# One more small load at the head of ScalarE's queue in a transformer layer of 256 tokens: columns of w_in into an unused tile

## The chip, the cores and the metric

One core of a Trainium2 chip. The metric is the kernel's time on the device in microseconds, the median of several runs; less is better. The kernel before takes 307.39 us (three runs, 307.19 to 308.2).

## What is computed

One decoder layer in float32, for a sequence of 256 tokens and 1024 features: a root-mean-square norm, attention with 16 heads of 64, a residual, a second norm, a squared-ReLU network of width 4096, a residual and a last norm. With 256 tokens the block-sparse attention of the reference has a single block, so that it is plain causal attention with a bias by distance. The reference, cut to this case:

```
y = rmsnorm(x, norm_mix)
q, k, v = split(y @ w_in, 3)                 # w_in: 1024 x 3072, float32
s = q @ k.T * 64 ** -0.5 + rel_bias[bucket(t - s)]     # per head, causal
h = x + (softmax(s) @ v) @ w_out
h = h + square(relu(rmsnorm(h, norm_mlp) @ mlp_up)) @ mlp_down
out = rmsnorm(h, final_norm)
```

## The kernel before

Every engine has its program written out by hand, with semaphores between them. The weights (w_in 12 MB, w_out 4 MB, mlp_up and mlp_down 16 MB each) come in tiles of 1 MB into four slots of `raw`, loaded by SyncE's queue (`load`, L209). ScalarE rounds each tile to a high part (`w_hi`, L604), VectorE takes the rest (`w_lo`, L808), and TensorE multiplies high by high and low, and low by high. The attention goes in four chunks of four heads, the network in sixteen chunks of 256 columns.

The order at the start is what matters here. SyncE issues the first 128 rows of x in two halves (L215, semaphores `x_half`), then the first tile of w_in, the columns of v, in four pieces of 256 KB (L220, `v_piece`), with the other 128 rows of x (L218, `x_next`) between the second and third, and then the next tile in two halves (L222, L223) and whole tiles (L209). ScalarE issues three small loads before its first work: `mix_rows` (the gain of the first norm, 8 x 128, L689), `onehot_sb` (L690) and `rel_sb` (L691), both tables for the bias. Then it loads an activation table (L692), and squares x for the norm (L694, L697).

TensorE begins with three products of constants that nobody reads (`idle_product`, L528), each recorded as two passes. It transposes four blocks of x (L292, which waits for `x_half[0]`), then the gains (L287, which waits for `mix_loaded`), then four more blocks (`x_half[1]`). VectorE copies the turned gains to `mixT` (L997) and multiplies the transposed x by them into `yF` (L884). With `yF` and the first piece of w_in TensorE starts v's first tile (`v_first`, L340); the table product L328 and the norm's factor (L300) come between its steps.

Quoted, the start of ScalarE's program and the wait in TensorE's transposes:

```
nc.scalar.dma_start(mix_rows[:], norm_mix[0].rearrange("(k p) -> k p", p=P)).then_inc(mix_loaded, 16)
nc.scalar.dma_start(onehot_sb[:], bucket_onehot).then_inc(tables_loaded, 16)
nc.scalar.dma_start(rel_sb[:], rel_bias).then_inc(tables_loaded, 16)
nc.scalar.preload_act_table(ACT.Sqrt)
act.wait_ge(x_half[0], 16)
...
    if tb == 0 and k == 4:
        pe.wait_ge(mix_loaded, 16)
        nc.tensor.transpose(bank[MIX][:, 0:KB], mix_rows[:], ident[0:KB, 0:KB]).then_inc(mix_turned, 1)
```

Of the kernel before, what the change touches and what calls it, by code (L numbers as in the profile page):

```python
# [31 lines left out]
P = 128  # L32
D = 1024
# [50 lines left out]
def build(nc, x, rel_bias, norm_mix, norm_mlp, mlp_up, mlp_down, w_in, w_out, final_norm,  # L84
# [9 lines left out]
    with ExitStack() as ctx:  # L94
        def sb(name, shape, dt=F32):
            return ctx.enter_context(nc.sbuf_tensor(name, shape, dt))

        def sem(name):
            return ctx.enter_context(nc.semaphore(name))
# [16 lines left out]
        oT = sb("oT", [P, PAIRS, 2, T], F32R)  # L116
        yF = sb("yF", [P, KB, T])
        warm = sb("warm", [P, 256])
        part = sb("part", [P, 2, T])
        z_sb = sb("z_sb", [P, 2, T])  # L120
        s_sb = sb("s_sb", [P, 2, T])
# [40 lines left out]
        bias_summed, bias_vec, bias_stored = sem("bias_summed"), sem("bias_vec"), sem("bias_stored")  # L162
        v_piece = [sem(f"v_piece{i}") for i in range(PIECES - 1)]
        q_first, fill_loaded, yf_done = sem("q_first"), sem("fill_loaded"), sem("yf_done")
        warm_made, sd_done = sem("warm_made"), sem("sd_done")
        square0_act, eps_made = sem("square0_act"), sem("eps_made")
        diag_done, spread_done, yn_done, ylo0_pool = sem("diag_done"), sem("spread_done"), sem("yn_done"), sem("ylo0_pool")
        hi_done, lo_done = sem("hi_done"), sem("lo_done")
# [18 lines left out]
        def cols(slot_tensor, slot):  # L187
            return slot_tensor[:, slot, :].rearrange("p (k n) -> p k n", k=KB)
# [13 lines left out]
        @block.sync  # L202
        def _(sp):
            def load(slot, src, split):

                if split is not None:
                    sp.wait_ge(lo_done, split)
                n = CE // src.shape[1]
                nc.sync.dma_start(raw[:, slot, :].rearrange("p (k n) -> p k n", n=n), src  # L209
                                  ).then_inc(raw_full[slot], 16)  # L210


            for b in range(2):
                own = slice(b * 512, (b + 1) * 512)
                nc.sync.dma_start(h_sb[:, 0, own], x_rows[0][:, own]).then_inc(x_half[b], 16)  # L215
            for i in range(PIECES):
                if i == 2:
                    nc.sync.dma_start(h_sb[:, 1, :], x_rows[1]).then_inc(x_next, 16)  # L218
                ks = slice(i * KB // PIECES, (i + 1) * KB // PIECES)
                nc.sync.dma_start(cols(raw, 0)[:, ks, :], w_in_v[:, ks, 2 * D:2 * D + CW]  # L220
                                  ).then_inc(v_piece[i] if i < PIECES - 1 else raw_full[0], 16)
            nc.sync.dma_start(cols(raw, 1)[:, 0:4, :], w_in_v[:, 0:4, 0:CW]).then_inc(q_first, 16)  # L222
            nc.sync.dma_start(cols(raw, 1)[:, 4:8, :], w_in_v[:, 4:8, 0:CW]).then_inc(raw_full[1], 16)  # L223
            for t, (c, part) in enumerate(IN_PARTS):
                if t > WHOLE:
                    own = slice(PART_BASE[part] + c * CW, PART_BASE[part] + (c + 1) * CW)
                    if t == SLOTS:
                        sp.wait_ge(unit_done, TB)
                    load(t % SLOTS, w_in_v[:, :, own], 2 * (t - SLOTS - WHOLE) + 2 if t > SLOTS else None)
            for q in range(CHUNKS_OUT):  # L230
                load(q, w_out_v[:, 2 * q:2 * q + 2, :], 2 * (OUT0 + q - SLOTS - WHOLE) + 2)
            with sp.Fori(0, CHUNKS_UP // 2) as i:
                for r in range(2):
                    load(2 * r, up_v[:, :, bass.ds(i * 2 * CW + r * CW, CW)], 8 * i + SPLIT0 - 6 + 4 * r)
                    load(2 * r + 1, down_v[:, bass.ds(i * 4 + 2 * r, 2), :], 8 * i + SPLIT0 - 4 + 4 * r)
            for tb in range(TB):
                for b in range(2):
                    own = slice(b * 512, (b + 1) * 512)
                    sp.wait_ge(out_ready, 2 * tb + b + 1)
                    nc.sync.dma_start(out_rows[tb][:, own], y_sb[:, tb, own]).then_inc(stored, 16)  # L240
            sp.wait_ge(stored, 16 * 2 * TB)
            sp.wait_ge(bias_stored, 16)


        @block.gpsimd
# [350 lines left out]
        def _(act):  # L596
# [77 lines left out]
            def h_hi(f, par, i):  # L674
                act.wait_ge(s_done, 2 * f + i + 1)
                nc.scalar.copy(hT[:, par, i, HI, :], s_sb[:, i, :]).then_inc(hhi_done, 1)  # L676

            def step(f, par, first=False, last=False):
# [4 lines left out]
                for i in range(2):  # L683
# [2 lines left out]
                        hi_mlp(f + 2, par, 0, i, (up_done, 2 * f + 2))  # L686
                    h_hi(f + 1, 1 - par, i)

            nc.scalar.dma_start(mix_rows[:], norm_mix[0].rearrange("(k p) -> k p", p=P)).then_inc(mix_loaded, 16)  # L689
            nc.scalar.dma_start(onehot_sb[:], bucket_onehot).then_inc(tables_loaded, 16)  # L690
            nc.scalar.dma_start(rel_sb[:], rel_bias).then_inc(tables_loaded, 16)  # L691
# [36 lines left out]
            for c in range(1, CHUNKS_IN):  # L728
                a, t = c - 1, 3 * c + 3
# [24 lines left out]
            a = CHUNKS_IN - 1  # L754
# [370 lines left out]
```

## Time and profile before

| | |
|---|---|
| median of 3 runs | 307.39 us (307.19 to 308.2) |
| the profiled execution | 306.87 us |
| its span, first to last instruction | 305.1 us |
| busy: TensorE, VectorE, ScalarE | 295.0, 205.8, 158.1 us |
| bytes moved | 55.86 MB, mean 183 GB/s |
| first product with weights (L340) | starts at 6.09 us |

The page is of one execution. Times in a view count from the first instruction of the span. Instructions that issue a transfer have an engine name with a q (ACTq, SPq); a transfer's landing is the moment when its semaphore is full. In the time lines a row merges neighbouring instructions of one line; "x6" is how many, and the brackets tell how long the engine idled before, and what ended that.

### The profile page before, as it was taken

To read this page: it belongs to the slowest core of one execution; us is meant where nothing else is said; L and a number is where in the kernel's file an instruction comes from. 1 tells how busy PE (TensorE), PEld (TensorE's weight loads), DVE (VectorE), ACT (ScalarE), POOL (GpSimd) and SP (SyncE) were. 2 spreads that over 40 slices of the span, in tenths; PEclk is the share of its full clock that TensorE was granted. 3 is DMA by queue.
4 is the path that set the end of the run, shared out by engine and by line. 5 is a ranking of instruction groups with operands and counts; after the bars stand their busy time and mean duration, and the time that the engine had idled before them with its cause. 6 is when DMAs were issued, how large, how long until landed. Compare 5 with 4: busy or idle time off the path is not lost.

```text
span 305.1 us, 4557 instructions
## 1 busy us (share of the span) xinstructions
PE 295.0 (97%) x1645; PEld 251.4 (82%) x1645; DVE 205.8 (67%) x396; ACT 158.1 (52%) x291; POOL 8.4 (3%) x15
## 2 busy tenths in 40 slices
PE   7979989999999999999999999999999999999992
PEld 5868888898997787888888888888888888888881
DVE  2696985984875757894674675666567467466564
ACT  3694753944935545745544545346355354444422
POOL 0401000000000000000000000000000000000000
PEclk9999999999999999999999999999999999999997
DMA  6999977257166044486566547647457556620003
GB/s 231 353 348 354 354 236 265 81 146 268 70 187 227 0 140 138 175 267 183 195 213 178 202 172 221 190 148 259 143 171 242 146 195 209 182 93 0 0 3 136
DMA packets 36685, 55.86 MB, mean 183 GB/s; under 512 B 1144, under 2 KB 29888, under 8 KB 36672
## 3 DMA queue, kind: packets, MB, share of 16 engines
q1 hardware_dynamic: 35632, 52.43, 53.2%
q0 software_dynamic: 928, 3.20, 2.9%
q8 instruction: 8, 0.13, 0.2%
q10 hardware_dynamic: 112, 0.06, 0.1%
q14 instruction: 5, 0.04, 0.0%
HBM read 54.61 MB, written 1.07 MB: 182 GB/s over the span
## 4 chain that ended last, share of the span: by engine, by line
PE 89%; DVE 4%; ACT 3%; DMA 1%; issue 1%; SPq 0%; DVEq 0%; ACTq 0%
PE bank L442 36%; PE bank L391 25%; PE bank L398 13%; PE bank L353 2%; PE bank L354 2%; PE bank L355 2%; PE bank L418 2%; PE bank L340 2%; DVE w_lo L808 2%; DMA raw<-in_a_w_in_dram 1%; PE bank L494 1%; PE bank L432 1%; ACT w_hi L604 1%; PE bank L410 1%; PE bank L408 1%
## 5 line engine op out<-in xcount | busy, mean ns | idle before, releaser
L808 DVE TENSOR_TENSOR w_lo<-raw,w_hi 128x1024 fp32r<-128x1024 f32 x94 | 112.8, 1221 | 40.6 <-ACT w_hi L604 39.5
L604 ACT CAST w_hi<-raw 128x1024 fp32r<-128x1024 f32 x93 | 95.3, 1052 | 32.7 <-PE bank L442 32.6
L391 PE MATMUL bank<-yT,w_hi 128*128 128x512 f32 x352 | 85.8, 392 | 2.4 <-DVE qT L904 2.4
L391 PEld LDWEIGHTS bank<-yT,w_hi 128*128 128x128 f32 x352 | 65.0, 188 | 16.6 <-issue 2.0
L442 PE MATMUL bank<-w_hi,hT 128*128 128x512 f32 x256 | 71.8, 390 | 0.0
L442 PEld LDWEIGHTS bank<-w_hi,hT 128*128 128x128 f32 x256 | 47.1, 188 | 9.0
L398 PEld LDWEIGHTS bank<-yT,w_lo 128*128 128x128 f32 x352 | 46.2, 191 | 2.4
L398 PE MATMUL bank<-yT,w_lo 128*128 128x256 f32 x352 | 46.9, 282 | 0.0
L442 PE MATMUL bank<-w_lo,hT 128*128 128x512 f32 x128 | 40.2, 390 | 0.0
L672 ACT COPY part<-bank 128x256 f32<-128x256 f32 x32 | 11.9, 370 | 36.7 <-PE bank L398 36.7
L442 PEld LDWEIGHTS bank<-w_lo,hT 128*128 128x128 f32 x128 | 24.0, 188 | 5.2
L974 DVE TENSOR_TENSOR z_sb<-bank,part 128x256 f32<-128x256 f32 x32 | 13.5, 422 | 20.3 <-ACT part L672 20.2
L676 ACT CAST hT<-s_sb 128x256 fp32r<-128x256 f32 x32 | 13.1, 408 | 15.2 <-DVE s_sb L976 15.2
L442 PE MATMUL bank<-w_hi,oT 128*128 128x512 f32 x64 | 19.8, 399 | 0.0
L660 ACT ACTIVATE probs<-probs,negmax 128x128 f32<-128x128 f32 (+1 forms) x32 | 14.2, 447 | 10.2 <-DVE negmax L913 10.1
L913 DVE CUSTOM_DVE_ANT_0 probs<-bank,bias_sb 128x128 f32<-128x128 f32 (+1 forms) x32 | 9.7, 350 | 8.1 <-PE bank L410 8.1
L981 DVE TENSOR_TENSOR hT<-s_sb,hT 128x256 fp32r<-128x256 f32 x32 | 13.5, 420 | 1.9 <-ACT hT L676 1.9
L976 DVE SCALAR_TENSOR_TENSOR s_sb<-z_sb 128x256 f32<-128x256 f32 x32 | 13.6, 425 | 1.1
L442 PEld LDWEIGHTS bank<-w_hi,oT 128*128 128x128 f32 x64 | 11.7, 188 | 3.0 <-issue 0.8
L353 PE MATMUL bank<-w_hi,yT 128*128 128x256 f32 x48 | 13.7, 285 | 0.0
L354 PE MATMUL bank<-w_lo,yT 128*128 128x256 f32 x48 | 13.6, 283 | 0.0
L355 PE MATMUL bank<-w_hi,yT 128*128 128x256 f32 x48 | 13.6, 283 | 0.0
(95 smaller groups left out, 238.5 us busy)
## 6 DMA issues: line engine op xcount, KB each, us to landing
raw<-in_mlp_up_dram SPq DMA_DIRECT2D x16, 1024.0 KB, 5.5
raw<-in_mlp_down_dram SPq DMA_DIRECT2D x16, 1024.0 KB, 4.9
raw<-in_a_w_in_dram SPq DMA_DIRECT2D x10, 1024.0 KB, 7.6
raw<-in_a_w_out_dram SPq DMA_DIRECT2D x4, 1024.0 KB, 4.9
bias_sb<-bias_by_distance POOLq DMA_DIRECT2D x4, 512.0 KB, 5.3
raw<-in_a_w_in_dram SPq DMA_DIRECT2D x4, 256.0 KB, 5.1
raw<-in_a_w_in_dram SPq DMA_DIRECT2D x2, 512.0 KB, 7.5
out_dram<-y_sb SPq DMA_DIRECT2D x4, 256.0 KB, 2.3
```

The lines of the kernel that those rows point to most:

```text
L353: mm(acc, yT[:, k, HI, tok], wh[:, k, :], start=(k == 0), stop=False)
L354: mm(acc, yT[:, k, HI, tok], wl[:, k, :], start=False, stop=False)
L355: last = mm(acc, yT[:, k, LO, tok], wh[:, k, :], start=False, stop=(k == KB - 1))
L391: mm(dst[:], wh[:, k, i * P:(i + 1) * P], yT[:, k, :, :], start=(k == 0), stop=False, skip_group_check=True)
L398: last = mm(dst[:, 0:T], wl[:, k, i * P:(i + 1) * P], yT[:, k, HI, :], start=False, stop=(k == KB - 1), skip_group_check=True)
L442: last = mm(bank[ACC[tb][c]][:], lhs(l), w[:, r, c * 512:(c + 1) * 512], start=first, stop=(stop and l == LO))
L604: nc.scalar.copy(w_hi[:, slot, part_of], raw[:, slot, part_of]).then_inc(hi_done, 1)
L660: last = nc.scalar.activation(probs[:, s, own], probs[:, s, own], ACT.Exp, bias=negmax[:, s, tb:tb + 1], scale=-1.0, accum_out=rowsum[:, s ...
L808: v.tensor_tensor(w_lo[:, slot, own], raw[:, slot, own], f32(w_hi[:, slot, own]), ALU.subtract).then_inc(lo_done, 1)
L974: v.tensor_tensor(z_sb[:, i, :], bank[UP[i]][:, 0:T], part[:, i, :], ALU.add).then_inc(z_done, 1)
L976: v.scalar_tensor_tensor(s_sb[:, i, :], z_sb[:, i, :], 0.0, z_sb[:, i, :], ALU.max, ALU.mult).then_inc(s_done, 1)
L981: v.tensor_tensor(hT[:, par, i, LO, :], s_sb[:, i, :], f32(hT[:, par, i, HI, :]), ALU.subtract).then_inc(hT_ready, 1)
```

## The change

It adds one load as the first on ScalarE's queue. It reads 16 columns (64 bytes), from column 2048 on, of rows 0, 4, 8, ... of w_in: 256 runs of 64 bytes, 16 KB, two of them to each of the 128 partitions of a new tile `touch` that nothing reads. SyncE waits for its semaphore at the very end. The three loads that stood first on the queue follow it; no other instruction moves. The rows of w_in are 12 KB long, so that the runs lie 48 KB apart and span the whole array.

```diff
+        touch = sb("touch", [P, 2, 16])
...
-        warm_made, sd_done = sem("warm_made"), sem("sd_done")
+        warm_made, sd_done, touched = sem("warm_made"), sem("sd_done"), sem("touched")
...
             sp.wait_ge(bias_stored, 16)
+            sp.wait_ge(touched, 16)
...
+            every_fourth = w_in[0].rearrange("(p a r) n -> p a r n", a=2, r=4)[:, :, 0, 2 * D:2 * D + 16]
+            nc.scalar.dma_start(touch[:], every_fourth).then_inc(touched, 16)
             nc.scalar.dma_start(mix_rows[:], norm_mix[0].rearrange("(k p) -> k p", p=P)).then_inc(mix_loaded, 16)
```

ScalarE's program at its start, before the change:

```order
0 L595 UNCONDITIONAL_BRANCH
1 L689 DMA mix_rows<-in_norm_mix_dram 8x128
2 L690 DMA onehot_sb<-in_bucket_onehot_dram 32x384
3 L691 DMA rel_sb<-in_rel_bias_dram 32x16
4 L692 ACT_TABLE_LOAD
5 L694 ACTIVATE squares,stat<-h_sb 128x512
```

The same place with the change:

```order
0 L597 UNCONDITIONAL_BRANCH
1 L692 DMA touch<-in_a_w_in_dram 128x2x16
2 L693 DMA mix_rows<-in_norm_mix_dram 8x128
3 L694 DMA onehot_sb<-in_bucket_onehot_dram 32x384
4 L695 DMA rel_sb<-in_rel_bias_dram 32x16
5 L696 ACT_TABLE_LOAD
6 L698 ACTIVATE squares,stat<-h_sb 128x512
```

The load of `touch` stands ahead of the others, and everything behind it has moved down by one; the lines of the file are two or four higher.

## Rows read from the trace of the kernel before

**Rows 1.** The page: busy time by engine, and the chain by engine.
```profile
PE 295.0 (97%) x1645; PEld 251.4 (82%) x1645; DVE 205.8 (67%) x396; ACT 158.1 (52%) x291; POOL 8.4 (3%) x15
...
PE 89%; DVE 4%; ACT 3%; DMA 1%; issue 1%; SPq 0%; DVEq 0%; ACTq 0%
```

**Rows 2.** The chain in order of time: start us, us, what.
```profile
1.27 0.42 SPq L215
1.69 0.05 issue
1.74 4.21 DMA raw<-in_a_w_in_dram
5.95 0.14 issue
6.09 1.10 PE bank L340 x4
...
12.68 0.23 PE bank L300 x2
12.91 0.02 issue
12.94 0.70 DVE y_sb L876
```

**Rows 3.** Time line of ScalarE: start us, us, instruction [idle before].
```profile
0.81 0.60 ACTq L689 DMA_DIRECT2D mix_rows<-in_norm_mix_dram  x1
1.80 0.43 ACTq L691 DMA_DIRECT2D rel_sb<-in_rel_bias_dram  x1
2.26 1.28 ACT L692 ACT_TABLE_LOAD   x1 [2.26 <-issue]
3.56 0.63 ACT L694 ACTIVATE squares<-h_sb 128x512 f32<-128x512 f32 x1
4.09 0.19 ACT L694 ACTIVATION_READ_ACCUMULATOR squares<-h_sb 128x1 f32 x1
4.86 0.63 ACT L697 ACTIVATE squares<-h_sb 128x512 f32<-128x512 f32 x1 [0.58 <-DMA h_sb<-in_x_dram]
```

**Rows 4.** Time line of TensorE's products.
```profile
1.27 2.93 PE L528 MATMUL bank<-warm 128*128 128x256 f32 x6 [1.27 <-DVE warm L993]
3.99 0.91 PE L292 MATMUL bank<-ident,h_sb 128*128 128x128 f32 x4
4.83 0.22 PE L287 MATMUL bank<-ident,mix_rows 8*128 8x8 f32 x1
4.98 0.66 PE L292 MATMUL bank<-ident,h_sb 128*128 128x128 f32 x4
6.09 1.10 PE L340 MATMUL bank<-raw,yF 128*128 128x256 f32 x4 [0.45 <-DMA raw<-in_a_w_in_dram]
7.12 0.81 PE L328 MATMUL bank<-onehot_sb,rel_sb 32*16 32x384 f32 x2
7.86 1.13 PE L340 MATMUL bank<-raw,yF 128*128 128x256 f32 x4
...
9.05 1.04 PE L292 MATMUL bank<-ident,h_sb 128*128 128x128 f32 x8
...
9.92 2.76 PE L340 MATMUL bank<-raw,yF 128*128 128x256 f32 x12
```

**Rows 5.** Time line of VectorE, and the tile yF.
```profile
5.17 0.17 DVE L997 COPY mixT<-bank 128x8 f32<-128x8 f32 x1 [3.94 <-PE bank L287]
5.25 0.14 DVE L999 TENSOR_SCALAR stat<-stat 128x1 f32<-128x1 f32 x1
5.37 1.35 DVE L884 TENSOR_TENSOR yF<-bank,mixT 128x256 f32<-128x256 f32 x3
...
L884 DVE TENSOR_TENSOR yF<-bank,mixT x3: 414/424/681, 5.4 to 6.0; 128x256 f32<-128x256 f32 x2, 128x512 f32<-128x512 f32 x1
```

**Rows 6.** Issues: SyncE's, landings of h_sb, onehot_sb and rel_sb (KB, us to landing).
```profile
0.82 0.87 SPq L215 DMA_DIRECT2D h_sb<-in_x_dram  x2
1.74 0.94 SPq L220 DMA_DIRECT2D raw<-in_a_w_in_dram  x2
...
DMA to landing us min/median/max: 2.7/3.6/5.6
...
onehot_sb<-in_bucket_onehot_dram ACTq DMA_DIRECT2D x1, 48.0 KB, 3.1
...
rel_sb<-in_rel_bias_dram ACTq DMA_DIRECT2D x1, 2.0 KB, 3.9
```

**Rows 7.** ScalarE's queue (q10): packets, MB, share; 1.5:2.6, 2.8:4.0, 4.0:6.0 us.
```profile
q10 hardware_dynamic: 16, 0.00, 1.5%
...
q10 hardware_dynamic: 46, 0.05, 15.9%
...
q10 hardware_dynamic: 50, 0.00, 1.8%
```

**Rows 8.** Stretches: us, busy per engine, PEclk, DMA share, GB/s.
```profile
3.50:4.50 1.00, 1.00 (x5) 0.70 (x4) 0.00 (x0) 0.77 (x3) 0.00 (x0) 1.00 0.72 191
...
5.50:6.50 1.00, 0.55 (x4) 0.42 (x3) 1.00 (x3) 0.38 (x2) 0.00 (x0) 1.00 1.08 377
...
8.50:9.50 1.00, 1.00 (x10) 0.95 (x9) 0.25 (x1) 1.00 (x2) 0.68 (x1) 1.00 1.08 381
```

## The prediction

> **What bounds the kernel now.** I read the page's chain first, since a small load can only matter where something waits for it. The chain is TensorE work for 89% of the span, and DMA has 1% [rows 1]. In order of time, that 1% is one piece: the first 256 KB of w_in, issued at 1.74 us and landed 4.21 us later, at 5.95 us [rows 2]. Behind it the products of L340 start at 6.09 us, and from there each piece of the chain is engine work that hangs on the one before: PE to 12.91, then DVE, ACT, and so on. No transfer is in the chain again in this stretch. So whatever moves the start of L340 should move the end by about as much, and a transfer that comes in later than it does now costs nothing until it passes the work that waits for it.
>
> The next views are the time lines of the three engines before 6.09 us. ScalarE issues three small loads from 0.81 us, loads a table until 3.54, squares the first half row of x from 3.56 to 4.28, then idles 0.58 us for the second half, until 4.86 [rows 3]. TensorE works on the unused products of L528 until about 4.0, starts the first four transposes at 3.99, turns mix_rows at 4.83, starts four more transposes at 4.98, and L340 at 6.09 [rows 4]. VectorE copies mixT at 5.17 and makes the first yF at 5.37; it has three of those, the short ones 0.41 to 0.42 us each, so the first is done near 5.8 [rows 5]. Two things therefore meet before L340: the weights at 5.95 and yF at about 5.8. They lie 0.15 us apart.
>
> **The change, part by part.** It removes and moves no computation. It adds one issue at the head of ScalarE's queue, its packets, and a last wait on SyncE.
>
> *The issue.* The load has 128 x 2 runs of 64 bytes, 256 in all, the same number of runs as the 256 KB pieces of w_in, two of which take SyncE 0.94 us, so 0.47 us each [rows 6]. The first issue of ScalarE's queue takes 0.60 us though it has eight runs [rows 3]. The touch takes that place, so I bound it by 0.47 and 0.9 us and take 0.6. What is behind it on ScalarE moves by 0.35 to 0.6 us: mix_rows is issued near 1.4 instead of 0.81, the table load ends near 4.0 instead of 3.54, the first squares end near 4.75 instead of 4.28. The 0.58 us in which ScalarE waits for x at 4.86 covers this. Cost on the path: 0. If the cover were gone, the squares would feed VectorE's L999 at 5.25, and beyond a delay of about 0.6 us the path.
>
> *The packets.* The load goes over the same 16 engines that carry x and w_in. The small packets of ScalarE's queue between 4.0 and 6.0 us are rel_sb's 64-byte runs, the same size as the touch's: 50 packets have 1.8% of 16 x 2.0 us, 11.5 ns each. Between 2.8 and 4.0 us that queue has 46 packets, mostly onehot_sb's, at 15.9% of 16 x 1.2 us, 66 ns each [rows 7]. So 256 packets and their 16 signals cost each engine 272 x 11.5 / 16 = 0.2 us at the low end and 272 x 66 / 16 = 1.1 us at the high end. I take 0.3 us, close to the row with the same packet size. Who is late by it: the first half row of x lands at 0.82 + 2.7 = 3.5 us [rows 3, 6] while TensorE is on L528 until 3.99, so 0.45 us of it are hidden. The second half lands at 4.86, with its transposes at 4.98: these would start 0.2 us later, and they end at 5.64 today, 0.45 us before L340. Nothing shows. The first piece of w_in would land at 6.25 instead of 5.95, and this does show: +0.3 us.
>
> *What the touch may give back.* It reads from every fourth row of w_in, hence all over the array, before the pieces do. The first pieces come slowly: between 3.5 and 4.5 us the engines move 191 GB/s at a share of 0.72, against 377 GB/s between 5.5 and 6.5 and 381 between 8.5 and 9.5 [rows 8]. The missing bytes of that microsecond are 1.0 x (377 - 191) / 377 = 0.5 us of transfer. If the slowness belongs to the first reads of that array, the touch takes some of it on itself, ahead of the pieces. The trace cannot say so: it may as well be the order in which the transfers were issued. Bounds: 0 and -0.5 us for the landing. But yF at 5.8 allows L340 to start only some 0.2 us sooner than now. I take -0.2 of the 0.3 above.
>
> *mix_rows.* It is now behind the touch on its queue. Today its eight packets and their eight signals are through before 2.6 us, since the queue's 16 packets by then are theirs [rows 7]. Moved by 0.6 us of issue and 0.2 to 1.1 us of touch, they are through between 3.4 and 4.3. TensorE wants them at 4.83. The other row, onehot_sb with 3.1 us from issue to landing [rows 6], gives 1.4 + 3.1 + 0.2 to 1.1 = 4.7 to 5.6 us: up to 0.8 us late, and VectorE's mixT and yF, which wait for it, as late. Eight packets are nearer to their own row, so I take 0, and keep +0.8 as the upper end.
>
> The Trainium skill's page DMA: Bandwidth & Descriptors, Queues, rings and completion order, says that each DMA engine goes round robin over the queues with work. By that rule x would alternate with the touch, where I have charged x the touch's whole time. The Trainium skill's same page, Bandwidth, lists 4 KB in 64 packets at 0.68 us, 10.5 ns a packet, for GpSimd's loads; by this figure 256 packets would be an estimated 2.7 us in a row and mix_rows would be late by a few tenths. No row here has so many tiny packets in one load.
>
> *The rest.* rel_sb lands at 1.80 + 3.9 = 5.7 us and L328 reads it at 7.12 [rows 3, 4, 6]; 1.4 us of cover, against 0.8 at most. The wait of SyncE at the end is for a load that will be 300 us old: 0. The unused tile costs 128 bytes a partition.
>
> **Sum.** +0.3 - 0.2 + 0 = +0.1 us on a profiled execution of 306.87 us (span 305.1), which is 0.5 below the median of 307.39. On the median: 307.5 us. A difference under 0.3%, 0.9 us, cannot be told from none for this kernel.
>
> **The rivals.**
> 1. *mix_rows comes late (slower if late enough).* Its place is the wait before L287, its price one for one through mixT, yF and L340. At 5.6 us it gives +0.8 - 0.1, about 308.2, still inside 0.3%. It decides past 5.8 us: then TensorE has more than 0.9 us of idling. For it: it stands behind 256 packets on one queue. Against: its own packets are gone today 2.2 us before they are wanted. Chance 0.13, of which 0.05 lands beyond 0.3%.
> 2. *TensorE's clock rises later (slower).* The first 256-column products cost 2.93 / 6 = 0.49 us each, those from 9.92 us 2.76 / 12 = 0.23; eight transposes take 1.04 us at 9.05, where the first four alone take 0.91 [rows 4]. So the engine starts at the lower of its two levels, 1.2 GHz, and rises to 2.4 between 4 and 5 us, after being busy since 1.27 without a gap. If x lands more than 0.45 us late, a gap opens at 4.0, and the rise may be put off. From 4.98 to 8.99 stand 0.66 + 1.10 + 0.81 + 1.13 = 3.7 us of work that would take up to twice as long; half of this stretch gives +1.8, less 0.3 of idling that absorbs it: about 308.9 us. It decides from a gap at 4.0 us that keeps the clock low. Chance 0.08. The Trainium skill's TensorE: Matmul & The Clock Gate, Part 1, adds that the chip's looks at activity are not tied to a kernel's start, so the same start may rise earlier or later by chance; the sum would not change by it.
> 3. *The touch pays (faster).* First pieces of w_in land up to 0.5 us sooner. VectorE's yF then caps the gain near 0.2 us, 307.2 us. To pass 0.3%, the later stages would have to wait for DMA too, and the chain holds 1% of DMA, all in that one piece. Chance 0.15, of which 0.04 for more than 0.3%.
> 4. *It does nothing*: the load runs wholly in gaps, or ahead of everything; 307.4 us. Chance 0.14.
>
> The forecast itself has a chance of 0.50.
>
> **How the numbers follow.** 307.5 us. Below, -0.2 from rival 3 and 0.5 for how single medians fall: 306.8. Above, rival 1 at its end and part of rival 2: 308.8. The runs shown span 307.19 to 308.2, so the width is mostly theirs. Faster: 0.04. Slower: 0.05 + 0.08 + 0.01 for a stray median = 0.14. Same: 0.82.
>
> **What would show it.** Right: in the changed profile the first L340 starts between 5.9 and 6.4 us; L287 starts near 4.8; mixT follows it; L528 still runs into the transposes with no gap; ScalarE's idling before its second squares shrinks from 0.58 to about 0.1 us; the rest of the chain is the old one, shifted. Wrong: L287 waits for DMA (rival 1); twelve products of L340 not at 0.23 us at their first group (rival 2); or a start of L340 within 0.2 us of 6.09 and yet an end moved by over 0.9 us, which would mean that the stage behind it depends on the landings in a way that the chain hides.

## The result, and the profile after

The changed kernel takes 309.23 us (six runs, 309.03 to 313.3) against 307.26 us (six runs, 306.75 to 308.2): a ratio of 1.0102 with a 95% interval of 1.0062 to 1.0141. Two of the six runs, 313.16 and 313.3 us, raise that ratio (the last section comes back to them); the two medians alone stand at 1.0064. By them it is slower by 2 us, and outside the forecast range of 306.8 to 308.8. The profiled execution took 309.03 us where the one before took 306.87, and its span is 307.3 us where it was 305.1. So the 2.2 us between the two profiled executions lie inside the span.

The loss does not arise at the start, where the load is. The chain after, in order of time (start us, us, what):

```profile
5.25 0.78 PE bank L294 x4
6.03 0.01 issue
6.04 1.13 PE bank L342 x4
...
12.92 0.70 DVE y_sb L880
```

The first products with weights start at 6.04 us where they started at 6.09, and VectorE begins at 12.92 where it began at 12.94 [rows 2]. No DMA is left in this stretch of the chain. The two chains then run side by side, piece for piece, and the changed one stays 0.01 to 0.06 us ahead, until 128 us. The network begins there. Before:

```profile
128.62 3.69 PE bank L391 x16
132.32 1.91 PE bank L398 x16
134.23 5.47 PE bank L442 x24
139.70 3.63 PE bank L391 x16
143.32 1.91 PE bank L398 x16
145.24 5.47 PE bank L442 x24
...
288.34 10.92 PE bank L442 x48
```

After:

```profile
128.56 3.72 PE bank L393 x16
132.28 1.91 PE bank L400 x16
134.19 5.58 PE bank L444 x24
139.77 3.66 PE bank L393 x16
143.42 1.91 PE bank L400 x16
145.34 5.58 PE bank L444 x24
...
290.26 11.17 PE bank L444 x48
```

Each product has two operands: a stationary one of 128 columns, which the profile shows as a weight load of its own, 128x128 (PEld), and a moving one of 256 or 512. Each step of the network is a group of wide products of the first matrix, 512 columns of the moving operand yT (L391, now L393), narrow ones, 256 columns of it (L398, L400), and 24 products of the second matrix, with hT stationary and 512 columns of the weights moving (L442, L444). The 24 take 5.58 us where they took 5.47, the 16 take 3.66 where they took 3.63, so a step takes 11.15 us (5.58 + 3.66 + 1.91) instead of 11.01; the last 48 take 0.25 us more. The first chain reaches the last 48 at 288.34 us, the second at 290.26. These 1.92 us, and 0.25 on top, are the whole loss. The page says the same of the groups. Before, then after (busy us, mean ns of one):

```profile
L442 PE MATMUL bank<-w_hi,hT 128*128 128x512 f32 x256 | 71.8, 390 | 0.0
...
L442 PE MATMUL bank<-w_lo,hT 128*128 128x512 f32 x128 | 40.2, 390 | 0.0
...
L442 PE MATMUL bank<-w_hi,oT 128*128 128x512 f32 x64 | 19.8, 399 | 0.0
```

```profile
L444 PE MATMUL bank<-w_hi,hT 128*128 128x512 f32 x256 | 73.1, 395 | 0.0
...
L444 PE MATMUL bank<-w_lo,hT 128*128 128x512 f32 x128 | 40.5, 392 | 0.0
...
L444 PE MATMUL bank<-w_hi,oT 128*128 128x512 f32 x64 | 19.8, 399 | 0.0
```

The products that read hT are slower, and those of the same line that read oT are not. TensorE waits for nothing in either. What tells the two tiles apart in the diff is the declaration of `touch`: it stands between `warm` and `part`, so part, z_sb, s_sb, hT and all tiles behind them move up by 128 bytes in each partition, and oT, yT, raw, w_hi and w_lo stay. In the program as built, the tiles follow each other without gaps. All that TensorE's wide products read (yT, w_hi, w_lo, oT, hT) start at 128 modulo 256 bytes before the change, that is, their address divided by 256 leaves 128; hT starts at 0 modulo 256 after it.

At the start, what the prediction asked to look at. ScalarE after:

```profile
0.83 0.64 ACTq L692 DMA_DIRECT2D touch<-in_a_w_in_dram  x1
1.50 0.74 ACTq L693 DMA_DIRECT2D mix_rows<-in_norm_mix_dram  x1
...
3.17 1.28 ACT L696 ACT_TABLE_LOAD   x1 [3.17 <-issue]
4.46 0.63 ACT L698 ACTIVATE squares<-h_sb 128x512 f32<-128x512 f32 x1
...
5.09 0.61 ACT L701 ACTIVATE squares<-h_sb 128x512 f32<-128x512 f32 x1
```

And the DMA view after: ScalarE's queue between 2.8 and 4.0 us, and the landing of the touch.

```profile
q10 hardware_dynamic: 280, 0.02, 20.1%
...
touch<-in_a_w_in_dram ACTq DMA_DIRECT2D x1, 16.0 KB, 3.1
```

In [rows 3] the table load began at 2.26 and ScalarE idled 0.58 us before its second squares; now it begins at 3.17, and the idling is gone. In [rows 7] the queue had 16 packets between 1.5 and 2.6 us; now it has none there, and its 280 between 2.8 and 4.0 us are nearly all the touch's (256 runs and 16 signals), 13.8 ns each (20.1% of 16 x 1.2 us over 280).

### The profile page after: what moved, and what is told of

It is laid out like the page before. It is cut to its first block, busy times and chain, and to the rows that moved or that the text cites. A ratio compares the mean times of both kernels' runs of the same rounds, so it can differ in the third digit from the quotient of the medians.

```text
span 307.3 us, 4558 instructions
## 1 busy us (share of the span) xinstructions
PE 297.6 (97%) x1645; PEld 251.8 (82%) x1645; DVE 205.8 (67%) x396; ACT 157.5 (51%) x291; POOL 8.4 (3%) x15
## 4 chain that ended last, share of the span: by engine, by line
PE 91%; DVE 4%; ACT 3%; issue 1%; DVEq 0%; ACTq 0%
PE bank L444 36%; PE bank L393 25%; PE bank L400 13%; PE bank L355 2%; PE bank L356 2%; PE bank L357 2%; PE bank L420 2%; PE bank L342 2%; DVE w_lo L812 2%; PE bank L496 1%; PE bank L434 1%; ACT w_hi L606 1%; PE bank L530 1%; PE bank L412 1%; PE bank L294 1%
## 5 line engine op out<-in xcount | busy, mean ns | idle before, releaser
L393 PE MATMUL bank<-yT,w_hi 128*128 128x512 f32 x352 | 86.3, 393 | 2.3 <-DVE qT L908 2.3
L393 PEld LDWEIGHTS bank<-yT,w_hi 128*128 128x128 f32 x352 | 64.9, 188 | 17.2 <-issue 2.0
L444 PE MATMUL bank<-w_hi,hT 128*128 128x512 f32 x256 | 73.1, 395 | 0.0
L444 PEld LDWEIGHTS bank<-w_hi,hT 128*128 128x128 f32 x256 | 47.2, 189 | 9.8
L400 PEld LDWEIGHTS bank<-yT,w_lo 128*128 128x128 f32 x352 | 46.2, 191 | 2.4
L400 PE MATMUL bank<-yT,w_lo 128*128 128x256 f32 x352 | 46.9, 282 | 0.0
L444 PE MATMUL bank<-w_lo,hT 128*128 128x512 f32 x128 | 40.5, 392 | 0.0
L444 PEld LDWEIGHTS bank<-w_lo,hT 128*128 128x128 f32 x128 | 24.1, 188 | 5.7
L444 PE MATMUL bank<-w_hi,oT 128*128 128x512 f32 x64 | 19.8, 399 | 0.0
L444 PEld LDWEIGHTS bank<-w_hi,oT 128*128 128x128 f32 x64 | 11.7, 188 | 3.0 <-issue 0.8
L355 PE MATMUL bank<-w_hi,yT 128*128 128x256 f32 x48 | 13.7, 285 | 0.0
L357 PE MATMUL bank<-w_hi,yT 128*128 128x256 f32 x48 | 13.6, 283 | 0.0
```

Of the source, the lines that this page charges most:

```text
L355: mm(acc, yT[:, k, HI, tok], wh[:, k, :], start=(k == 0), stop=False)
L357: last = mm(acc, yT[:, k, LO, tok], wh[:, k, :], start=False, stop=(k == KB - 1))
L393: mm(dst[:], wh[:, k, i * P:(i + 1) * P], yT[:, k, :, :], start=(k == 0), stop=False, skip_group_check=True)
L400: last = mm(dst[:, 0:T], wl[:, k, i * P:(i + 1) * P], yT[:, k, HI, :], start=False, stop=(k == KB - 1), skip_group_check=True)
L444: last = mm(bank[ACC[tb][c]][:], lhs(l), w[:, r, c * 512:(c + 1) * 512], start=first, stop=(stop and l == LO))
```

## The experiments

The theories after the result. *Place*: the tile, not the load, costs the 2 us, because hT is moved. *Load*: the transfer, its issue or the longer program costs them, in a way that the chain does not show.

**The tile without the load.** The tile as in the change, none of its other lines.

```diff
         warm = sb("warm", [P, 256])
+        touch = sb("touch", [P, 2, 16])
         part = sb("part", [P, 2, T])
```

> The unused tile of 128 bytes a partition stands where the change put it, but there is no load and no wait. Theory 'place' (the tile moves part, z_sb, s_sb, hT and all later tiles up by 128 bytes, and the products L444 that read hT get slower, 24 in 5.58 us where they were 24 in 5.47): 309.2 us, the products at 5.58 again. Theory 'load' (the transfer, its issue or the longer program costs the 2 us): 307.3 us and 5.47.

Measured: 309.64 us, ratio 1.0072 (1.0055 to 1.0089), and 24 products in 5.58 us again:

```profile
144.26 3.66 PE bank L392 x16
...
149.83 5.58 PE bank L443 x24
```

Its profiled execution took 313.52 us; the last section shows where that time went.

**The load with the tile last.** The whole change, `touch` declared behind `stat`.

```diff
-        touch = sb("touch", [P, 2, 16])
...
         stat = sb("stat", [P, 6, 6])
+        touch = sb("touch", [P, 2, 16])
```

> The whole change, but with the tile declared last, so that no other tile moves. Theory 'place': 307.3 us or, by the earlier start of the first products, 0.1 less; 24 products in 5.47 us. Theory 'load': 309.2 us and 5.58.

Measured: 307.45 us, ratio 1.0012 (0.9993 to 1.0031), 24 products in 5.47 us:

```profile
145.24 5.47 PE bank L444 x24
150.71 3.63 PE bank L393 x16
```

These two runs settle it between the theories: the tile's place costs the 2 us, and the load costs nothing inside the span, whose median is 305.15 us in these ten runs and 305.4 in the nineteen of the kernel before beside them. But four of the ten took 307.9 to 308.5 and one 308.83. In these five, 2.5 to 2.9 us of the time lie outside the span, and in the other five 1.7 or 1.8. The same was seen without the load, 2.5 us in two of the nineteen runs before and in the single run with hT moved by 256 bytes below, and in none of the six runs of the change itself. What this extra microsecond is, and whether the load makes it more frequent, was not shown.

**Which of the moved tiles.** A pad of 128 bytes behind s_sb moves hT and not part, z_sb and s_sb. With hT declared first, and the pad before `part`, these three stand off and hT does not. The tiles declared behind them all (`gain` and on) stand off by 128 bytes in both kernels.

```diff
         s_sb = sb("s_sb", [P, 2, T])
+        pad = sb("pad", [P, 32])
         hT = sb("hT", [P, 2, 2, 2, T], F32R)
```

> No load; a pad of 128 bytes stands between s_sb and hT, so that hT and what is behind it move and part, z_sb and s_sb do not. Theory 'place, hT': 309.2 us. Theory 'place, part/z_sb/s_sb' (ScalarE's and VectorE's accesses to these slow TensorE down): 307.3 us. Theory 'load': 307.3.

```diff
+        hT = sb("hT", [P, 2, 2, 2, T], F32R)
+        pad = sb("pad", [P, 32])
         part = sb("part", [P, 2, T])
...
-        hT = sb("hT", [P, 2, 2, 2, T], F32R)
```

> No load; hT is declared before the pad and part, z_sb and s_sb behind it, so that these three lie 128 bytes off (and 8 KB up) while hT keeps its place modulo 2048 bytes. Theory 'place, hT': 307.3 us. Theory 'place, part/z_sb/s_sb': 309.2 us. Theory 'load': 307.3.

Measured: 309.47 us, ratio 1.0074 (1.0052 to 1.0097), for hT; 307.01 us, ratio 0.9995 (0.9986 to 1.0005), for the others. The 24 products, with hT off and then with the others off:

```profile
146.07 5.58 PE bank L443 x24
```

```profile
145.09 5.47 PE bank L443 x24
```

It is hT. The tiles behind it are off in the fast kernel too, and so are ruled out.

**How far.** The same pad with other sizes (16 columns, as shown, are 64 bytes; 64 and 256 columns are 256 and 1024), and the output projection's tile oT moved by 1024 bytes (with a second pad, so that what is behind moves by 2048).

```diff
         s_sb = sb("s_sb", [P, 2, T])
+        pad = sb("pad", [P, 16])
         hT = sb("hT", [P, 2, 2, 2, T], F32R)
```

> Pad of 64 bytes before hT. Theory 'same offset' (fast only where hT stands at the same place modulo 512 bytes as the tiles of weights, all of which stand at 128 modulo 512): slow, 24 products in 5.58 us, about 309.3 us. Theory 'steps of 128' (only whole 128-byte lines count): fast, 5.47 us and 307.2.

> Pad of 256 bytes before hT. Theory 'same offset modulo 512': slow, 5.58 us, 309.3. Theory 'same offset modulo 256': fast, 5.47 us, 307.2.

> Pad of 1024 bytes before hT. Theory 'same offset modulo 512 (or 256)': fast, 5.47 us, 307.2. Theory 'modulo 2048' (the output projection reads oT, which stands where hT would now, modulo 2048, and its products take 9.07 us for 39, 233 ns each, against 228 for hT): slow, 5.58 us or more, 309.3.

```diff
+        pad = sb("pad", [P, 256])
         oT = sb("oT", [P, PAIRS, 2, T], F32R)
+        pad2 = sb("pad2", [P, 256])
         yF = sb("yF", [P, KB, T])
```

> Pads of 1024 bytes before oT and before yF, so that oT moves by 1024 and everything behind it by 2048 bytes. Theory 'same offset modulo 512': nothing changes, 39 products of L442 in 9.07 us, 307.2. Theory 'modulo 2048': these 39 in 8.85 us, the output projection about 0.4 us shorter in all, 306.8; the products of the network stay at 24 in 5.47.

One profiled run each. The group of 24 in the chain, for 64, 256 and 1024 bytes:

```profile
145.74 5.60 PE bank L443 x24
```

```profile
145.57 5.47 PE bank L443 x24
```

```profile
145.87 5.47 PE bank L443 x24
```

The times were 309.56, 307.96 and 307.49 us, beside 307.08 for the kernel before; spans 307.8, 305.5 and 305.8. So 64 and 128 bytes are slow, 0, 256 and 1024 fast: as far as these sizes tell, the place counts modulo 256. My guesses of 512 and of 2048 both fell. With oT moved by 1024 the time was 307.14 us, and its 39 products in a row took 9.07 us as before, 233 ns each. Their mean misled me. In the kernel before, the last 26 of them, from 111.07 to 116.96 us, take 227 ns each like those that read hT; only the first 13 take 237. Why these do is open.

**Who meets whom.** To part TensorE's read of hT from the writes of ScalarE and VectorE, the second product reads another tile, while they write hT as before. In the first of two kernels hT is off by 128 bytes and the read goes to oT, which is not; in the second oT is off and hT is not. Both compute with the attention's output in place of the activations, so their results are not the layer's; they serve for the time alone.

```diff
-                    last = accumulate(lambda l: hT[:, par, i, l, tb * P:(tb + 1) * P], 2 * par + 1, i, tb,
+                    last = accumulate(lambda l: oT[:, 2 * par + i, l, tb * P:(tb + 1) * P], 2 * par + 1, i, tb,
```

> hT is off by 128 bytes, and ScalarE and VectorE write it there as before, but the second product of the network reads its stationary operand from oT (of the same strides, in its old place): it computes with the attention's output in place of the activations. Theory 'TensorE's weight load reads a tile that is off': fast, 24 products in 5.47 us, 307.2. Theory 'the writers' (ScalarE and VectorE, writing hT, get in TensorE's way): slow, 5.58, 309.3.

> The other way round: oT is off by 128 bytes, hT keeps its place (modulo 2048), and the second product reads from oT, again the attention's output in place of the activations. Theory 'weight load': slow, 5.58 us; and the output projection, which reads oT too, is slower as well: its 96 products some 4 ns each, 0.4 us, so about 309.5 us in all. Theory 'writers': fast in the network, 5.47, 307.2.

Measured, one run each, beside 307.09 us for the kernel before: 307.12 us and 309.54 us. The network's group in the first:

```profile
145.50 5.47 PE bank L443 x24
```

In the second the output projection slows as well; its 39 products took 9.07 us before. Here, with the network's group:

```profile
108.30 9.28 PE bank L444 x39
...
145.85 5.58 PE bank L444 x24
```

So it is TensorE's own read of the stationary operand, whichever tile that is, and no other engine's access.

**Against what.** One kernel moves all tiles together, by a pad before the first; one moves only yT, the moving operand of the first product, and keeps the rest in place modulo 256.

```diff
+        pad = sb("pad", [P, 32])
         h_sb = sb("h_sb", [P, TB, D])
```

> A pad of 128 bytes before the first tile, so that every tile moves by as much, and the places relative to each other stay. Theory 'relative' (the stationary and the moving operand must stand at the same place modulo 256 bytes): fast everywhere, 5.47 and 3.63 us, 307.2. Theory 'absolute' (a tile at 0 modulo 256 is slow, at 128 fast): slow everywhere, 24 products in 5.58 us, 16 of L391 in more than 3.66, and the attention too: more than 309.3 us.

```diff
+        pad = sb("pad", [P, 32])
         yT = sb("yT", [P, KB, 2, T], F32R)
+        pad2 = sb("pad2", [P, 32])
         raw = sb("raw", [P, SLOTS, CE])
```

> Pads of 128 bytes before yT and before raw: yT is off by 128 modulo 256 from the tiles of weights, and all else, raised by 256, keeps its place among the others. Theory 'relative' (any pair of stationary and moving operand that is off is slow): the first product of the network, 16 of L391 with yT moving, takes more than 3.63 us, some 4 ns each more, and so do the 96 wide products of the attention; 352 products together 1.5 us: 308.6 us; the second product stays near 5.47. Theory 'only a stationary operand that is off by itself': 307.2.

Measured: 307.05 us with all moved, in one run, and the 24 products take 5.47 us again. With yT moved, 308.31 us (eight runs, 308.15 to 308.65; ratio 1.0028, 0.9995 to 1.0061). The interval includes 1, but the eight lie closely together, 1.2 us above the median of 307.11 us of the nineteen runs before, one of which took 311.2. And now the other group is slow:

```profile
139.92 3.73 PE bank L393 x16
143.64 1.90 PE bank L400 x16
145.54 5.47 PE bank L444 x24
```

16 take 3.73 us instead of 3.63, 24 take 5.47. It is the place of the stationary operand against the moving one, modulo 256 bytes, and not a place by itself. It shows in products with 512 moving columns only: the 16 narrow ones (L400), whose moving yT is off just the same, take 1.90 us against 1.91, and the 256-column products of the attention that have yT stationary (L353 to L355, here L355 to L357) have means of 281 to 283 ns against 283 to 285.

**Is there a gain left?** In the kernel before, ident and diag stand 32 bytes off, behind the 32-byte mixT. Declared last, mixT leaves them in line.

```diff
-        mixT = sb("mixT", [P, KB])
...
         stat = sb("stat", [P, 6, 6])
+        mixT = sb("mixT", [P, KB])
```

> mixT, 32 bytes, is declared last, so that diag and ident come to 128 modulo 256 like the operands that they meet; in the kernel before they stand 32 bytes off. Theory 'relative': the 64 transposes, which move ident, get shorter: 12 of L418 take 1.31 us, 109 ns each; at most 5 ns each, 0.3 us in all: 306.9 us. If the transposes are bounded by something else: 307.2.

Measured: 307.2 us, ratio 0.9992 (0.9963 to 1.0021), and 12 transposes (L418) still take 1.31 us. Either the 128-column products do not show the effect, or 32 bytes do not. No version beat the kernel before.

**The load, four times as large.** Tile last; 64 bytes of every row.

```diff
-            every_fourth = w_in[0].rearrange("(p a r) n -> p a r n", a=2, r=4)[:, :, 0, 2 * D:2 * D + 16]
-            nc.scalar.dma_start(touch[:], every_fourth).then_inc(touched, 16)
+            every_row = w_in[0].rearrange("(p a) n -> p a n", a=8)[:, :, 2 * D:2 * D + 16]
+            nc.scalar.dma_start(touch[:], every_row).then_inc(touched, 16)
```

> The change with its tile last and four times the runs: 64 bytes of every row of w_in, 1024 of them. By the prediction's terms the issue takes 0.64 us for 256 runs, so some 1.5 to 2.5 us, and the table load ends about 1.2 to 1.9 us later, past 5.6 us; mix_rows is issued near 3 us and lands after 5 us, so that the transposes at 4.98 and everything behind them are 0.5 to 1.5 us late: 307.7 to 308.7 us. If the gap on TensorE holds the clock down, as in a run of the kernel with the unused tile alone (rise at 14.3 us, 313.5 us), up to 312. If the load costs nothing that shows: 307.3.

Measured: 310.93 us (four runs, 308.29 to 311.24), ratio 1.0101 (1.0052 to 1.015). Three of the runs have spans of 309.0 to 309.5 us; the fourth has 305.5, so the loss inside the span is not there in every run. The chain of the profiled execution, which is one of the three:

```profile
0.83 0.64 ACTq L692
...
1.50 3.65 DMA mix_rows<-in_norm_mix_dram
...
5.19 0.28 PE bank L289
...
6.58 2.04 PE bank L342 x4
```

The issue takes 0.64 us for 1024 runs as for 256, so my term by the number of runs was wrong. What is late is mix_rows, landed at 5.15 us behind the runs, and L289 waits for it; this is rival 1. The first products start 0.5 us late, and the four take 2.04 us where they took 1.10 [rows 2]: the clock is still low, which is rival 2. VectorE's y_sb, at 12.94 us before, comes at 16.82. So of 3.9 us, 0.5 are the late start and 3.4 the clock.

## Why the prediction was wrong

- **The failed step** is a half sentence under "The rest": "The unused tile costs 128 bytes a partition." It was put at nothing without a reason. What the runs showed in its place: the tile moves hT, the stationary operand of 384 products on the chain, by half of 256 bytes against their moving operand: +0.11 us per group of 24 and +0.03 on the group of 16 behind it, fourteen times, and +0.25 on the last 48, 2.2 us in all. The forecast was for no change, and no rival had this.
- **The sum for the load, +0.1 us, held in its total.** With the tile out of the way the load measures +0.4 us with an interval of -0.2 to +1.0. Its parts did not all hold, as follows, so that the total is right in part by luck. In the profiled run of the change L342 starts 0.05 us sooner, which says little: in the twelve profiled kernels without the load, the one of the last section left out, it starts anywhere from 5.91 to 6.40 us.
- *The issue*: taken at 0.6 us, measured 0.64. The knock-on was larger than given, since mix_rows took 0.74 us to issue instead of 0.60: the table load ended 0.9 us later, past the 0.35 to 0.6 forecast. The first squares ended near 5.2 us, which used up the idling of 0.58. Nothing came of it, because VectorE wanted them only at 5.45.
- *The packets*: 11.5 ns taken, 13.8 measured. But they did not stand ahead of x: they passed between 2.8 and 4.0 us, and x's first half landed 2.7 us after its issue as before. The first piece of w_in landed 4.1 us after its issue, against 4.2, so the +0.3 us for it never came.
- *What it gives back*: -0.2 us was taken. The engines move 281 GB/s between 3.5 and 4.5 us against 191 before [rows 8]. With the tile last it is 273, and in the thirteen profiled kernels without a load it is 156 to 256, so the touch may well give something back; one run of each does not show it, and four times the load has 198. What there was is masked by the work before L342, whose transposes, at the lower clock, end at 6.03. That no product waits for weights is not the load's doing: of the thirteen, only the kernel before has that wait.
- *mix_rows*: L289 came at 4.98 instead of 4.83, behind transposes that took 1.06 us instead of 0.91 [rows 4], not behind its transfer. The load is not the cause, for with the tile alone they took 1.06 us and L288 came at 4.98 too. The value 0 was right.
- **Rival 2** was priced at +1.8 us and did not cause this result. The late clock itself exists, at a higher price: 3.4 us with four times the load and 4.4 in the last section. That a gap on TensorE brings it about is not shown (see there).
- *The closing test* said that a start within 0.2 us of 6.09 and an end moved by over 0.9 would mean a hidden dependence on landings. The condition was met (6.04 against 6.09 us, and an end 2 us later), and the reading was wrong: I had allowed only for waits, not for instructions that get longer by themselves.

## What to carry to other kernels

A declared tile is an edit to every tile behind it. When a change that should cost nothing costs a steady per cent, compare the mean of equal instructions in both traces before looking for a wait, and test the tile and the work apart. For wide products like these, keep the operands that TensorE reads together at the same place modulo 256 bytes; declaring small, odd-sized tiles last does that.

## What was not expected of the hardware

Wide products (128 x 512, 5.47 / 24 = 228 ns apart) come to 5.58 / 24 = 232.5 ns, 2% more, when the stationary operand stands 128 bytes off the moving one modulo 256; at 64 bytes it is 5.60 us, at 256 or 1024 nothing. Products with 256 moving columns do not show it. Why was not shown; only that it hangs on the pair.

The first microseconds can cost more than any of this. In the profiled run of the tile without the load (313.52 us) the second half of x landed 4.92 us after its issue, at 6.19 us; in the kernel before that took until 4.86 [rows 3]. TensorE after that landing:

```profile
6.23 1.12 PE L293 MATMUL bank<-ident,h_sb 128*128 128x128 f32 x4 [0.98 <-DMA h_sb<-in_x_dram]
7.14 1.92 PE L341 MATMUL bank<-raw,yF 128*128 128x256 f32 x4
...
10.38 2.08 PE L341 MATMUL bank<-raw,yF 128*128 128x256 f32 x4
...
12.68 1.85 PE L293 MATMUL bank<-ident,h_sb 128*128 128x128 f32 x8
14.36 2.75 PE L341 MATMUL bank<-raw,yF 128*128 128x256 f32 x12
```

TensorE idled 0.98 us and then ran at the lower level, 1.2 GHz, until about 14.3 us: four products in 2.08 us against 1.13, eight transposes in 1.85 against 1.04 [rows 4]. Then the twelve take 2.75 us, as before. The start of this group is 4.4 us late, and VectorE's y_sb, at 17.37 us instead of 12.94, is as late. The level is read from the lengths of the products: the granted clock in the profile's rows is 1.00 in every microsecond from 0 to 16, in this run and in the kernel before. Whether the idling kept the clock down was not shown. In the profiled run with four times the load, idling of only 0.15 us before L289 went with a rise about as late, between 12.5 and 14.0 us; in the one with hT moved by 256 bytes, idling of 0.22 us before 5.46 us went with the four products in 1.17 us at 6.37, so without a late rise. Two of the six runs of the change, at 313.16 and 313.3 us, have spans of 311.4 and 311.6 us and fit this, though they were not profiled; in two series of nineteen runs of the kernel before, beside the experiments, one each took 311.57 and 311.2. That the load makes it more frequent cannot be told: one of five runs with the tile alone had it too, and with the load and the tile last, none of ten did. Four times the load had it in three of four runs.
